# Two of 22 gate/up units left plain instead of six, the others as seven block products with the row factor applied to the results

## The reference

```python
FFN_HIDDEN = 2816                                   # 22 tiles of 128
x = x + merged @ w_o
h2 = rmsnorm(x, norm2_g)        # x * rsqrt(mean(x*x) + eps) * norm2_g, per token
g_ff, up_ff = jnp.split(h2 @ w_gate_up, 2, axis=-1)
return x + (jax.nn.silu(g_ff) * up_ff) @ w_down
```

## Time and profile before

| | |
|---|---|
| median of 3 runs | 1312.52 us |
| profiled execution, its time | 1312.36 us |
| its span, first to last instruction | 1310.6 us |
| PE busy | 1303.3 us (99%) |
| DVE, ACT, POOL busy | 654.8, 552.5, 646.9 us |
| granted TensorE clock | 0.999 of full |
| seven-product groups | 550.05 to 630.68 us, and a second of the same length |

### The profile page before, as it was taken

How to read it: one execution, slowest core, us unless ns; L and a number is a source line. 1 busy time by engine, 2 the same in 40 slices (tenths; PEclk the granted TensorE clock), 3 DMA queues, 4 the chain that set the end, 5 groups by cost and what they waited for, 6 DMA issues and landing times.

```text
span 1310.6 us, 17996 instructions
## 1 busy us (share of the span) xinstructions
PE 1303.3 (99%) x7064; PEld 1095.7 (84%) x7064; DVE 654.8 (50%) x1065; ACT 552.5 (42%) x848; POOL 646.9 (49%) x480
## 2 busy tenths in 40 slices
PE   9999999999999999999999999999999999999998
PEld 8877877787888888899899988877778888888887
DVE  3674544556454466776147644766544322342233
ACT  6223533566433443544234345345555224342333
POOL 4463333434553466887568753543334453335441
PEclk9999999999999999999999999999999999999999
DMA  6333152413222332333333342332321232323221
GB/s 205 97 114 104 41 153 60 134 41 121 81 73 97 97 97 73 115 103 116 110 97 97 97 161 81 109 92 79 97 65 65 97 96 79 115 65 111 99 79 65
DMA packets 143611, 126.89 MB, mean 97 GB/s; under 512 B 4464, under 2 KB 138736, under 8 KB 143536
## 3 DMA queue, kind: packets, MB, share of 16 engines
q1 hardware_dynamic: 143184, 125.66, 31.4%
q10 hardware_dynamic: 352, 0.19, 0.1%
HBM read 120.46 MB, written 2.10 MB: 94 GB/s over the span
## 4 chain that ended last, share of the span: by engine, by line
PE 99%; ACT 0%; ACTq 0%; DVE 0%; issue 0%
PE gemm L706 22%; PE gemm L707 22%; PE gemm L714 22%; PE gemm L1021 4%; PE gemm L1017 4%; PE gemm L1016 4%; PE gemm L764 2%; PE gemm L763 2%; PE gemm L767 2%; PE gemm L730 2%; PE gemm L731 2%; PE gemm L736 2%; PE mix L1145 1%; PE mix L1133 1%; PE mix L1122 1%; PE mix L1199 1%
## 5 line engine op out<-in xcount | busy, mean ns | idle before, releaser
L583 POOL TENSOR_TENSOR wlo<-raw,whi 128x512 fp32r<-128x512 f32 x360 | 493.6, 1403 | 434.3 <-ACT whi L1297 434.3
L706 PE MATMUL gemm<-hh,whi 128*128 128x512 f32 x872 | 344.3, 395 | 0.0
L707 PE MATMUL gemm<-hl,whi 128*128 128x512 f32 x872 | 339.8, 390 | 0.0
L714 PE MATMUL gemm<-hh,wlo 128*128 128x512 f32 x872 | 217.0, 390 | 0.0
L1297 ACT ACTIVATE whi<-raw 128x2048 fp32r<-128x2048 f32 x90 | 171.9, 1910 | 87.7 <-PE gemm L714 56.3
L706 PEld LDWEIGHTS gemm<-hh,whi 128*128 128x128 f32 x872 | 163.8, 188 | 38.0 <-issue 4.2
L707 PEld LDWEIGHTS gemm<-hl,whi 128*128 128x128 f32 x872 | 163.8, 188 | 33.1 <-issue 0.2
L714 PEld LDWEIGHTS gemm<-hh,wlo 128*128 128x128 f32 x872 | 163.3, 188 | 33.6
L579 POOL TENSOR_TENSOR wlo_b<-raw_b,whi_b 128x512 fp32r<-128x512 f32 x16 | 20.7, 1291 | 145.1 <-ACT whi L1297 145.1
L612 POOL TENSOR_TENSOR wlo<-raw,whi 128x512 fp32r<-128x512 f32 x48 | 61.7, 1302 | 9.1 <-ACT whi L1500 9.1
L1017 PE MATMUL gemm<-hs_lo,whi 128*128 128x256 f32 x256 | 64.2, 283 | 0.0
(11 more groups left out here) (495 smaller groups left out, 2486.3 us busy)
## 6 DMA issues: line engine op xcount, KB each, us to landing
raw<-w_in SPq DMA_DIRECT2D x53, 1024.0 KB, 5.3
raw<-w_gu SPq DMA_DIRECT2D x44, 512.0 KB, 5.1
raw<-w_o SPq DMA_DIRECT2D x8, 1024.0 KB, 5.3
raw<-w_down SPq DMA_DIRECT2D x16, 512.0 KB, 4.4
raw_b<-w_branch SPq DMA_DIRECT2D x16, 256.0 KB, 5.7
raw<-w_ao SPq DMA_DIRECT2D x4, 1024.0 KB, 5.1
raw<-w_so SPq DMA_DIRECT2D x4, 1024.0 KB, 5.3
raw<-w_in SPq DMA_DIRECT2D x7, 512.0 KB, 4.0
```

The source lines that it names most:

```text
L583: last = nc.gpsimd.tensor_tensor(a(wlo), a(raw), as_f32(a(whi)), ALU.subtract)
L706: mm(bank[:, :], w, xh[:, k, :], start=(k == 0), stop=False)
L707: mm(bank[:, :], w, xl[:, k, :], start=False, stop=False)
L714: last = mm(bank[:, :], wlo_[:, s, k, col:col + P], xh[:, k, :], start=False, stop=(k == kts - 1))
```

## The change

- `FFN_PARTS` becomes 8, 8, 6. The first part keeps two plain units and has six seven-product units; the parts behind have eight and six. That is 2 plain units and 20 of seven products.
- The inputs of the seven products are not normalized: `hh`, `hl` themselves serve for the three plain inputs, and `hn` = xT * norm2_g is made by ACT, eight copies of 512 columns, in the last four units before the network (the `w_o` units). Its four sums `t_sum` (DVE), their high parts `t_hi` (ACT) and rests `t_lo` (DVE) are made at once behind it, ahead of the results of the first plain unit.
- Since `R` is not in the inputs, DVE multiplies gate and up by `R` for each seven-product unit, behind the last addition (`scaled_sums`, two instructions of 512 columns, all operands in SBUF).
- `xhi`, `xlo` are gone. The seven weight blocks of a unit lie once in `whi`/`wlo` (four in one slot, three in the other), and a block is refilled for the next unit as soon as PE has used it. The product order is A11, A12, S1, A22, S2, S3, S4, and the splits of the next unit wait for the single products (`part_ps`).
- Some semaphores are merged (`acc`, `gate_act`, `st_vec`), and the split of the second plain unit's weights moves ahead of the row factor on ACT.

The diff, cut to its core:

```diff
-FFN_PARTS = (6, 8, 8)
+FFN_PARTS = (8, 8, 6)
...
-        hs_hi = place("hs_hi", [P, 7, 4, HALF], 76, f32r)
-        hs_lo = place("hs_lo", [P, 7, 4, HALF], Z0 + 36, f32r)
-        xhi = place("xhi", [P, 2, 3, 512], 48, f32r)
-        xlo = place("xlo", [P, 2, 3, 512], Z0 + 75, f32r)
+        t_sum = [place(f"t_sum{i}", [P, 4, HALF], at) for i, at in enumerate((48, 52, 56, Z0 + 32))]
+        t_lo = [place(f"t_lo{i}", [P, 4, HALF], at, f32r) for i, at in enumerate((48, 52, 56, Z0 + 32))]
+        t_hi = place("t_hi", [P, 4, 4, HALF], Z0 + 36, f32r)
...
+                if u.first:
+                    pe.wait_ge(sem("tile_free"), T - 3)
                 else:
+                    pe.wait_ge(sem("c_sum"), 4 * w - 2)
+                pe.wait_ge(sem("s_hi"), 5 * w + 1)
+                product(bank(u, Y)[:, left], A11, 0, 2 * n + 1).then_inc(sem("part_ps"), 1)
...
+                product(bank(u, X)[:, right], A12, 1).then_inc(sem("part_ps"), 1)
+                pe.wait_ge(sem("tile_free"), T - 1)
+                pe.wait_ge(sem("s_lo"), 3 * w + 1)
+                if u.first:
+                    pe.wait_ge(sem("t_lo"), 4 * t_count(u))
+                product(bank(u, Z)[:, left], S1, 3).then_inc(sem("part_ps"), 1)
...
+                product(bank(u, W)[:, left], A22, 6, 2 * n + 2).then_inc(sem("part_ps"), 1)
+                pe.wait_ge(sem("s_lo"), 3 * w + 2)
+                product(bank(u, X)[:, left], S2, 4).then_inc(sem("part_ps"), 1)
                 pe.wait_ge(sem("p1_read"), w + 1)
                 pe.wait_ge(sem("s3_lo"), w + 1)
+                product(bank(u, Y)[:, right], S3, 5).then_inc(sem("tile_done"), 1)
+                pe.wait_ge(sem("s_lo"), 3 * w + 3)
+                product(bank(u, W)[:, right], S4, 2).then_inc(sem("tile_done"), 1)
...
+                for u, nx in zip(units, units[1:] + [None]):
+                    before = units[u.i - 1] if u.i else None
+                    sum_hi(u, S4)
+                    first_product(u)
+                    if before:
+                        after_1(before)
+                    if nx:
+                        first_his(nx)
+                        sum_hi(nx, S1)
+                    if before:
+                        after_2(before)
+                    if nx:
+                        fourth_hi(nx)
+                        sum_hi(nx, S2)
+                        sum_hi(nx, S3)
...
+            def scaled_sums(u):
+
+                dve.wait_ge(sem("tile_free"), u.T + 2)
+                for part in (gate_of(u), up_of(u)):
+                    tt(part, part, R[:, :], ALU.mult).then_inc(sem("c_sum"), 1)
```

More of the change, by code:

```diff
@@ L25 @@
 from contextlib import ExitStack
+from dataclasses import dataclass
 SEQ, DM = 512, 1024
@@ L74 @@
 RUNS = [(0, 0, 0, 512), (1, 0, 512, 384), (2, 0, 896, 256), (1, 384, 1152, 128)]
+@dataclass
+class Seven:
+    n: int
+    w: int
+    T: int
+    T0: int
+    base: int
+    kt: int
+    kind: str
+    i: int
+    first: bool
+    last: bool
 def build_program(nc, x, par, cst1, cst2a, w_in, w_branch, w_o, w_gu, w_down, w_in2, sg_w, sg_b, ln_g,
@@ L342, in build_program @@
         LAST = tiles_before(N_UNITS - 1)
[L344 to L349, removed]
-        U2, U3, U4 = 0, 1, 2
[L353 to L357, removed]
+        SEVEN = []
@@ new lines, in group, with hidden_of @@
+        def group(kind, n0, count, kt=4):
+            g = [Seven(n0 + i, len(SEVEN) + i, tiles_before(n0 + i), tiles_before(n0), n0 % 2, kt, kind, i, i == 0, i == count - 1)
+                 for i in range(count)]
+            SEVEN.extend(g)
+            return g
+        HIDDEN = [group("hidden", n0 + (0 if f else 2), part - (0 if f else 2)) for f, (n0, part, h0) in enumerate(ffn_units)]
+        def hidden_of(u):
+            return u.n - ffn_units[0][0] - sum(4 for n0, part, h0 in ffn_units if u.n >= n0 + part)
@@ new lines, in ffn_h0, with t_count, raw_block, blocks @@
+        def ffn_h0(u):
+            return max(h0 for n0, part, h0 in ffn_units if u.n >= n0)
+        def t_count(u):
+            return 1
+        def raw_block(u, f, k):
+            return raw[:, u.n % 2, k * u.kt:(k + 1) * u.kt, f * P:(f + 1) * P]
+        def blocks(t, slot, b, count=1):
+            flat = t[:, :, :, :].rearrange("p s k c -> p (s k c)")
+            at = (4 * slot + b) * 512
+            return flat[:, at:at + count * 512].rearrange("p (k c) -> p k c", c=P)
+        A11, A12, S1, A22 = 0, 1, 2, 3
@@ L486, in _ @@
                 half = part // 2
[L487 to L495, removed]
+                stream(n0, part, lambda u, slot: [(cols(w_gu, (u + h0) * P + c, P), raw[:, slot, :, at:at + P])
+                                                  for c, at in ((0, 0), (FFN, P))])
                 def down_from(c0):
@@ L604, in _ @@
             rests(n_b0, n_c0, True)
-            rests(n_c0, ffn_units[1][0])
+            rests(n_c0, HIDDEN[0][0].n)
             sub, mult = ALU.subtract, ALU.mult
[L609 to L617, removed]
@@ L634, in hidden, with plain_rest @@
[L634 to L640, removed]
-            for f, (n0, part, h0) in enumerate(ffn_units):
[L642 to L659, removed]
+            def plain_rest(u, b, f, k):
+                return nc.gpsimd.tensor_tensor(part_of(wlo, u, b), raw_block(u, f, k), as_f32(part_of(whi, u, b)), sub)
@@ new lines, in seven_group @@
+            def seven_group(units, after):
+                third_sum(units[0])
+                first_rests(units[0])
+                fourth_rest(units[0])
+                for u, nx in zip(units, units[1:] + [None]):
+                    third_rest(u)
+                    if nx:
+                        third_sum(nx)
+                    if u.i:
+                        after(units[u.i - 1])
+                    if nx:
+                        first_rests(nx)
+                        fourth_rest(nx)
+                    else:
+                        rest(u.n + 1, (u.n + 1) % 2)
+                after(units[-1])
@@ L660, in _ @@
+            for f, (n0, part, h0) in enumerate(ffn_units):
+                seven_group(HIDDEN[f], hidden)
+                rests(n0 + part + 1, HIDDEN[f + 1][0].n if f < len(FFN_PARTS) - 1 else n_e0)
             rests(n_e0, N_UNITS)
@@ L1002, in _, with seven_products, product @@
                 unit_fm(n_c0 + p, mh, ml)
-            def seven_products(w, T0):
-                n = SEVEN[w][0]
-                s, T = n % 2, tiles_before(n)
+            def seven_products(u, x):
+                n, w, T = u.n, u.w, u.T
                 left, right = slice(0, HALF), slice(HALF, SEQ)
[L1010 to L1017, removed]
+                def product(o, b, xi, lo_ready=None):
+                    for k in range(u.kt):
+                        wk = part_of(whi, u, b)[:, k, :]
+                        mm(o, wk, x(xi, k)[0], start=(k == 0), stop=False)
+                        mm(o, wk, x(xi, k)[1], start=False, stop=False)
@@ L1018, in product @@
                     if lo_ready:
                         pe.wait_ge(sem("lo_done"), lo_ready)
-                    for k in range(4):
-                        last = mm(bank, lo[:, k * P:(k + 1) * P], hs_hi[:, x, k, :], start=False, stop=(k == 3))
-                    return last
[L1024 to L1031, removed]
+                    for k in range(u.kt):
+                        last = mm(o, part_of(wlo, u, b)[:, k, :], x(xi, k)[0], start=False, stop=(k == u.kt - 1))
@@ new lines, in first_his @@
+            def first_his(u):
+                act.wait_ge(sem(f"raw_in{u.n % 2}"), raw_count(u.n))
+                if u.first:
+                    act.wait_ge(sem("tile_done"), tiles_before(u.n - 1))
+                else:
+                    act.wait_ge(sem("part_ps"), 5 * u.w - 3)
+                for b in ((A11, A12) if u.kt < 4 else (None,)):
+                    if b is None:
+                        last = fn(blocks(whi, u.base, A11, 2), raw[:, u.n % 2, :, 0:P], ACT.Copy)
+                    else:
+                        last = fn(part_of(whi, u, b), raw_block(u, 0, b), ACT.Copy)
+                last.then_inc(sem("s_hi"), 1)
@@ new lines, in first_product, with split_after @@
+            def first_product(u):
+                act.wait_ge(sem("part_ps"), 5 * u.w + 1)
+                if u.w:
+                    act.wait_ge(sem("c_sum"), 4 * u.w - 3)
+                fn(p1_t[:, :], bank(u, Y)[:, 0:HALF], ACT.Copy).then_inc(sem("p1_read"), 1)
+            def split_after(u):
+                n = u.n + 1
+                act.wait_ge(sem(f"raw_in{n % 2}"), raw_count(n))
+                act.wait_ge(sem("part_ps"), 5 * u.w + 4)
+                fn(whi[:, n % 2], raw[:, n % 2], ACT.Copy).then_inc(sem("hi_done"), 1)
@@ L2192, in _, with seven_last @@
+            def seven_last(u):
+                at = 4 * (u.w % 2)
+                dve.wait_ge(sem("tile_free"), u.T + 1)
+                dve.wait_ge(sem("tile_done"), u.T + 2)
```

(3 more changed lines are left out.)

462 lines of the change are left out of this document (221 added, 241 removed).

## The result

The changed kernel takes 1316.53 us (median of 8 runs, 1316.36 to 1316.91) where the kernel before took 1312.66 on the same chip (1312.43 to 1313.39): a ratio of 1.0029, with an interval of 1.0018 to 1.0040. It is slower by about 3.9 us. The profiled execution took 1316.65, its span is 1314.7 against 1310.6, and the granted clock is 0.999, so PE runs at the upper of its two levels throughout. The forecast was 1316.2.

What follows compares the result with a forecast made beforehand. PE, busy for 1303.3 of 1310.6 us, was taken to bound the kernel. 1312.36 - 3.2 (saving) + 3.5 (boundaries) + 3.2 (start) + 0.2 (group ends) = 1316.1, forecast as 1316.2 for the median; range 1310 to 1322.

Steps and rivals of the forecast that it cites:

- The saving of 3.2 us: PE in the hidden stage: four plain units become seven-product units, from 10.88 to 10.08 us each, 3.2 us less.
- floor of 1309.2: Whole kernel: 1312.36 us less 3.2 us of PE time, since no other PE time can go.
- The walk of 10.3 us a unit: DVE per seven-product unit: 8.2 us alone, plus 0.8, 0.6, 0.3 and 0.4 for meetings with POOL and a wait.
- The term of 3.5 us: Unit boundaries within groups: DVE's walk over 10.08 us delays PE by 0.22 us at 16 of 17 boundaries.
- The start, 3.2 us: Start of the network: DVE's late sums and rests delay the second seven-product unit from 484.0 to 487.2; bounds 0 and 4.5.
- list of seven: DVE at the network's start: three sums and four rests of 1024 columns, slowed by POOL, end at about 471 us.
- 5.8 us to the second unit's start: DVE at the start, after 481.6: S4 rest, three sums, S1 rest, two additions and S2 rest take 5.8 us.
- The ends of groups, 0.2: Group ends: the last hidden tile's chain grows from 4.1 to 6 to 7 us, costing 0.2 us, up to 0.8.
- All hidden: Rival for the whole stage: DVE catches up in POOL's pauses and nothing is lost, 1309.3 us; chance 0.10.
- Only the start costs: Rival: a walk of 10.0 us suffices, so only the network's start loses time, 1312.7 us, no change; chance 0.25.
- The harder lock: Rival at unit boundaries: products by `R` always caught behind POOL, walk 11 then 10.8 us, 1324 us; chance 0.15.
- Late weights: Rival at unit boundaries: PE waits for the single weight copy, 0.5 us more at 17 boundaries, 1325 us; chance 0.05.

Runs made afterwards that it cites:

- last experiment: Changed kernel with `R` and the first and last input sums in PSUM, POOL's second-plain-unit rests waiting for all four sums; 1309.22 us, ratio 0.9973.
- both experiments in which no product is held up: Changed kernel with `R` copied to PSUM for the products, 1312.41 us; changed kernel with the products by `R` left out, 1312.43 us.

## Why the prediction was right

- *The saving of 3.2 us* is real: with the gaps gone the stage takes 3.18 us less than before. The last experiment's 1309.22 meets the prediction's floor of 1309.2, in part by luck: against the kernel before on its own chip it is 3.57 less, and 0.4 of that is not in this stage (the interval, 2.2 to 5.0, takes in both).
- *The walk of 10.3 us a unit* came out at 10.36, and its parts one by one. The weight sum from `raw` is held up by 0.79 (said 0.8), DVE stands still for 0.45 (0.6), the hidden tile's rest is held up by 0.35 (0.3), and the products with `R` by 0.24 and 0.81 in turn, 0.52 in the mean (0.4). That is 2.11 us against 2.1 on top of the 8.2. The term of 3.5 us measured 3.97, and both experiments in which no product is held up take 4.1 off (1312.41, 1312.43).
- *The pattern* was not foreseen: I spread the loss evenly over 16 boundaries at 0.22, and it is seven of about 0.54 with two small ones. The sum comes out near because the walks take turns, 10.08 and 10.65, and their mean of 10.36 is near the 10.3 forecast.
- *The start, 3.2 us,* measured 3.39. The list of seven ended at 470.68 (said 471), the third product began at 477.36 (477.5), the fifth at 481.59 (481.6), the second unit at 487.55 (487.2). Taking POOL's rests out took 3.1 us away. One step was loose: the 5.8 us to the second unit's start had no items, its rows without meetings add up to 4.9, and 481.6 + 5.8 is 487.4. It measured 6.0, since the first weight sum was held up by 1.13 there (1.82 at 482.05).
- *The ends of groups, 0.2,* measured 0.11.
- *The rivals.* All hidden is excluded by the gaps; its time is reached when the meetings that matter are taken away (1309.2, said 1309.3). Only the start costs is what the run with `R` in PSUM shows, a walk of 10.08 and 1312.41 (said 1312.7). The harder lock would have wanted 10.8 a unit; single products do take up to 1.81 us, but in turn with nearly free ones. Late weights: PE waits once for `wlo`, at the start, because DVE is behind there, and never again for any weight. The weights held once cost nothing.
- *What was too simple:* the prediction spoke of the added instructions as the cause. The kernel before with the same two products shows that they cost nothing while POOL pauses beside them and DVE has 0.7 us left.

By the Trainium skill (SBUF — State Buffer, Who interferes with whom) a DVE instruction with at most one SBUF input, outside the two-port modes, doesn't contend with GpSimd, while one with two contends with a GpSimd instruction that reads SBUF. The runs agree for `TENSOR_TENSOR`: 0.68 to 0.69 in 40 of 40 products once `R` lay in PSUM, 0.68 to 1.81 before. The prediction left out the condition on the modes. Nothing in its sum hangs on it, but see the first point of the last section.

## What to carry to other kernels

Where DVE and GpSimd both work through a stage, count DVE's walk over one unit and compare it with PE's time for it; here a mean busy share of 54% hid a walk of 8.2 of 10.08 us, to which meetings and a wait add 2.1. Before adding a DVE instruction with two SBUF inputs there, ask which GpSimd instruction stands beside it, and put the operand that is reused into an idle PSUM bank: one copy took 4.1 us away, with all work and its order kept. Where a long list of such instructions can't be moved, a wait that keeps GpSimd out of its first part may help: it was part of the last experiment, though its own share wasn't measured.

## What was unexpected

- A DVE instruction with a single SBUF input was also held up: the high part `ah<-fu_t` (TENSOR_SCALAR, SBUF to SBUF) took 1.40 us in the last experiment, with POOL at work, and 0.43 in the changed kernel at 478.80, where POOL starts its next one only at 479.05. The kernel before had it as well (1.41 at 464.88). So one SBUF input alone is no safeguard against POOL:

```profile
469.46 1.40 DVE L2194 TENSOR_SCALAR ah<-fu_t 128x512 fp32r<-128x512 f32 x1
```

- A wait of PE costs about 0.1 us more than itself: the second matmul behind it starts 0.22 after the first (603.30 to 603.52), the following ones 0.12 apart.
